# Attention: turned probabilities leave PSUM two chunks at a time, through two buffers of two banks in place of four of one

## What is computed

```
for blk in range(S // Q_BLOCK):                      # 16 blocks of 128 queries
    q0, q1 = blk * 128, blk * 128 + 128
    s = einsum("bhqd,bhkd->bhqk", q[:, :, q0:q1], k[:, :, :q1])
    s = s + cum[:, :, q0:q1, None] - cum[:, :, None, :q1]
    p = softmax(where(causal, s, -inf), axis=-1)
    outs.append(einsum("bhqk,bhkd->bhqd", p, v[:, :, :q1]))
```

## Time and profile before

| | |
|---|---|
| Median of three runs | 2558.09 us |
| Profiled execution, its own time | 2556.05 us |
| Its span, first to last instruction | 2553.9 us |
| Instructions | 37956 |
| TensorE matmul busy | 2409.2 us, 94% |
| TensorE weight load busy | 2081.5 us, 82% |
| DVE busy | 1352.8 us, 53% |
| ACT busy | 1150.0 us, 45% |
| POOL busy | 622.7 us, 24% |
| Mean granted TensorE clock | 0.974 |
| L828 on DVE, 640 instructions | 370.7 us busy |
| L773 on ACT, 640 instructions | 311.5 us busy |
| L692 on TensorE, 2176 instructions | 338.3 us busy |

### The profile page before, as it was taken

How to read it: one execution, slowest core, us unless ns; L and a number is a source line. 1 busy time by engine, 2 the same in 40 slices (tenths; PEclk the granted TensorE clock), 3 DMA queues, 4 the chain that set the end, 5 groups by cost and what they waited for, 6 DMA issues and landing times. The chain is left out here.

```text
span 2553.9 us, 37956 instructions
## 1 busy us (share of the span) xinstructions
PE 2409.2 (94%) x13921; PEld 2081.5 (82%) x13921; DVE 1352.8 (53%) x2844; ACT 1150.0 (45%) x2132; POOL 622.7 (24%) x739
## 2 busy tenths in 40 slices
PE   8999999999989999999999999699699999992997
PEld 7888889998868888888888888587488888872886
DVE  4232121211017888888888888453336656575443
ACT  2131111111117888888888888400035556565100
POOL 0010000000003554555545555244300000000254
PEclk9999999999998999999999999899899999996999
DMA  6434443332116455444554444455344444444653
GB/s 209 122 91 124 124 124 113 119 108 91 66 61 136 98 122 131 104 98 98 128 128 102 97 99 96 147 203 194 124 153 122 142 144 132 139 125 139 236 193 132
DMA packets 219999, 326.62 MB, mean 128 GB/s; under 512 B 17052, under 2 KB 144092, under 8 KB 213996
## 3 DMA queue, kind: packets, MB, share of 16 engines
q1 hardware_dynamic: 219304, 323.68, 44.3%
q0 software_dynamic: 512, 0.53, 0.1%
HBM read 197.79 MB, written 126.35 MB: 127 GB/s over the span
## 5 line engine op out<-in xcount | busy, mean ns | idle before, releaser
L828 DVE TENSOR_TENSOR at_pl<-at_tps,at_ph 128x512 fp32r<-128x512 f32 (+3 forms) x640 | 370.7, 604 | 30.1 <-ACT at_ph L773 30.1
L773 ACT ACTIVATE at_ph<-at_tps 128x512 fp32r<-128x512 f32 (+3 forms) x640 | 311.5, 527 | 114.5 <-PE at_tps L692 107.4
L323 ACT ACTIVATE pa_stg<-pa_ps 128x512 fp32r<-128x512 f32 (+1 forms) x128 | 76.5, 598 | 634.9 <-PE pa_ps L250 634.9
L692 PE MATMUL at_tps<-at_ident,at_probs 128*128 128x128 f32 x2176 | 338.3, 274 | 0.2 <-DVE at_pl L828 0.2
L710 PE MATMUL at_ops<-at_ph,at_val 128*128 128x256 f32 (+1 forms) x1152 | 325.5, 305 | 2.1 <-DVE at_pl L828 0.5
L763 ACT ACTIVATE at_probs<-at_probs,at_least 128x128 f32<-128x128 f32 (+15 forms) x256 | 307.2, 1200 | 9.1 <-DVE at_probs L819 9.0
L250 PE MATMUL pa_ps<-pa_xh,pa_wh 128*128 128x512 f32 x768 | 299.8, 390 | 3.8 <-DVE pa_wl L376 3.8
L250 PE MATMUL pa_ps<-pa_xh,pa_wl 128*128 128x512 f32 x768 | 298.9, 389 | 0.0
L250 PE MATMUL pa_ps<-pa_xl,pa_wh 128*128 128x512 f32 x768 | 298.8, 389 | 0.0
L710 PE MATMUL at_ops<-at_pl,at_val 128*128 128x256 f32 (+1 forms) x1152 | 295.0, 281 | 0.0
L677 PE MATMUL at_sps<-at_k,at_q 128*128 128x512 f32 (+3 forms) x640 | 272.9, 426 | 19.9 <-DMA at_k<-forget_sums 15.8
(11 more groups left out here) (172 smaller groups left out, 4645.4 us busy)
## 6 DMA issues: line engine op xcount, KB each, us to landing
at_q<-q_halves SPq DMA_DIRECT2D x45, 512.0 KB
at_k<-k_halves SPq DMA_DIRECT2D x45, 512.0 KB
q_halves<-pa_stg SPq DMA_DIRECT2D x32, 512.0 KB, 3.8
k_halves<-pa_stg SPq DMA_DIRECT2D x32, 512.0 KB, 3.7
v_halves<-pa_stg SPq DMA_DIRECT2D x32, 512.0 KB, 2.8
y_gated<-rep_work SPq DMA_DIRECT2D x32, 512.0 KB, 2.9
at_val<-v_halves SPq DMA_DIRECT2D x15, 1024.0 KB, 17.4
pa_wst<-in_attn_w_in SPq DMA_DIRECT2D x14, 1024.0 KB, 7.2
```

Of the source, the lines that this page charges most:

```text
L692: mm = nc.tensor.transpose(tps[c % TB][:, k, :], probs[s % ROWS][:, t0:t0 + P], ident[:, :])
L773: nc.scalar.activation(ph[g % 2][:, j * PB:j * PB + n, i % 2 * P:(i % 2 + 1) * P], tps[c % TB][:, 0:n, :], ACT.Copy).then_inc(high_out, 1)
L828: nc.vector.tensor_tensor(pl[g % 2][at], tps[c % TB][:, 0:n, :], raw(ph[g % 2][at]), ALU.subtract)\
```

## The change

A span is two chunks of a row, up to 1024 keys and eight tiles, and has one PSUM buffer of two banks; there are two such buffers in place of four of one bank. A row has one span (rows 0 to 7) or two (rows 8 to 15): 24 a head, 48 a pair. TensorE turns the tiles chunk by chunk in the same order as before, but it waits for the buffer once per span and counts `turned` up at the end of a span. `high` and `low` each handle a whole span in one instruction. DVE's order in a step changes: takes have the keys 0, 2, 4, 6 and lows 3, 7, so with four chunks it is take 0, take 1, low 0, take 2, take 3, low 1. The waits that counted chunks of `turned`, `high_out` and `low_out` count spans. The wait of the queue that loads a head is written in another way and has the same value.

```diff
+    n_spans = [(n + 1) // 2 for n in n_chunks]
+    first_span = [sum(n_spans[:s]) for s in range(STEPS)]
+    SPANS = sum(n_spans)
-    SB, TB = 2, 4
+    SB, TB = 2, 2
...
+    def span_tiles(s, j):
+        return min(2 * PB, s % QT + 1 - 2 * j * PB)
...
-        tps = [a.ps(f"tps{i}", [P, PB, P]) for i in range(TB)]
+        tps = [a.ps(f"tps{i}", [P, 2 * PB, P]) for i in range(TB)]
...
-                wait(sp, scored, chunks_before(it, QT * (hp + 1)) - CH if hp == 0 else it * CH)
+                wait(sp, scored, it * CH - CH // 2 if hp == 0 else it * CH)
...
-                c = first[s] + j
-                wait(pe, low_out, it * CH + c - TB + 1)
+                c = first_span[s] + j // 2
+                if j % 2 == 0:
+                    wait(pe, low_out, it * SPANS + c - TB + 1)
                 for k in range(width(s, j) // P):
                     t0 = (j * PB + k) * P
-                    mm = nc.tensor.transpose(tps[c % TB][:, k, :], probs[s % ROWS][:, t0:t0 + P], ident[:, :])
-                mm.then_inc(turned, 1)
+                    mm = nc.tensor.transpose(tps[c % TB][:, j % 2 * PB + k, :], probs[s % ROWS][:, t0:t0 + P], ident[:, :])
+                if j % 2 == 1 or j + 1 == n_chunks[s]:
+                    mm.then_inc(turned, 1)
...
-                    wait(pe, low_out, it * CH + first[2 * g + 1] + n_chunks[2 * g + 1])
+                    wait(pe, low_out, it * SPANS + first_span[2 * g + 1] + n_spans[2 * g + 1])
...
-                c, n = first[s] + j, width(s, j) // P
-                wait(act, turned, it * CH + c + 1)
-                nc.scalar.activation(ph[g % 2][:, j * PB:j * PB + n, i % 2 * P:(i % 2 + 1) * P],
+                c, n = first_span[s] + j, span_tiles(s, j)
+                wait(act, turned, it * SPANS + c + 1)
+                nc.scalar.activation(ph[g % 2][:, 2 * j * PB:2 * j * PB + n, i % 2 * P:(i % 2 + 1) * P],
                                      tps[c % TB][:, 0:n, :], ACT.Copy).then_inc(high_out, 1)
...
-                at(TURN_LAG, lambda t, n: [high(t, n, j) for j in range(n_chunks[n])])
+                at(TURN_LAG, lambda t, n: [high(t, n, j) for j in range(n_spans[n])])
...
-                    wait(dve, turned, chunks_before(it, s - ROWS + 1))
+                    wait(dve, turned, spans_before(it, s - ROWS + 1))
...
-                c, n = first[s] + j, width(s, j) // P
-                wait(dve, high_out, it * CH + c + 1)
-                at = (slice(None), slice(j * PB, j * PB + n), slice(i % 2 * P, (i % 2 + 1) * P))
+                c, n = first_span[s] + j, span_tiles(s, j)
+                wait(dve, high_out, it * SPANS + c + 1)
+                at = (slice(None), slice(2 * j * PB, 2 * j * PB + n), slice(i % 2 * P, (i % 2 + 1) * P))
...
-                turns = n_chunks[t_s] if turning else 0
-                for k, (second, j) in enumerate(alternate(scores_now, turns, 1)):
+                turns = n_spans[t_s] if turning else 0
+                order = sorted([(2 * j, False, j) for j in range(scores_now)]
+                               + [(4 * j + 3, True, j) for j in range(turns)])
+                for k, (_, second, j) in enumerate(order):
```

More of the change, by code:

```diff
@@ L481, in attend, with spans_before @@
     SKIP = 3
-    SB, TB = 2, 4
-    assert CH % SB == 0 and CH % TB == 0 and GROUPS % 4 == 0
-    def chunks_before(it, s):
-        return it * CH + first[s] if s >= 0 else it * CH - CH + first[s + STEPS]
+    SB, TB = 2, 2
+    assert CH % SB == 0 and SPANS % TB == 0 and GROUPS % 4 == 0
+    def spans_before(it, s):
+        return it * SPANS + first_span[s] if s >= 0 else it * SPANS - SPANS + first_span[s + STEPS]
+    def span_tiles(s, j):
+        return min(2 * PB, s % QT + 1 - 2 * j * PB)
     def width(s, j):
```

## The result

| | before | after |
|---|---|---|
| Median | 2558.18 us (4 runs) | 2611.24 us (4 runs) |
| Ratio | 1 | 1.0206, 95% interval 1.0188 to 1.0223 |
| Profiled execution, own time | 2556.05 us | 2607.12 us |
| Span | 2553.9 us | 2605.0 us |
| Attention, first to last matmul | 857.07 us | 908.67 us |

The change makes the kernel 53 us slower by the medians. Forecast were 2601 us, 43 us slower, in a range of 2578 to 2618. In the two traces attention grows by 51.6 us and the span by 51.1: the loss lies there and nowhere else.

What follows compares the result with a forecast made beforehand. TensorE, busy 94% of the span, was taken to bound the kernel. Terms a to h summed to +2.69 us a head, +43 us over 16 heads, giving 2601 us in a range of 2578 to 2618.

Steps and rivals of the forecast that it cites:

- Rival 1: Fewer instructions shorten the queue before takes, and TensorE's waits of 1.3 us a head go: at best 2537 us; 7%.
- rival 3: The wide instructions cost like two narrow ones: 2612 us, inside the range; 10% of the chance is there.
- Rival 2: Only the end of a head hurts (e to g): 2585 us; 12%.
- a: Step 12, first transposes: wait for the first wide low of step 11 to free the buffer, +0.5 us a head.
- b: Step 13, first score: waits for the third take of step 12, delayed behind a wide low, +0.36 us a head.
- c: Step 14, first score: waits likewise for the third take of the step before, +0.13 us a head.
- d: Step 16, third chunk's transposes: wait for the second low of step 15, +0.1 us a head.
- e: Step 17, first transposes: wait for step 16's first low, late through ACT's chain from step 15's exponential, +1.1 us a head.
- f: Step 18, first transposes: wait for the first low of step 17, +0.1 us a head.
- g: Step 19, weigh: waits for all of row 15, whose last wide high and low end later, +0.5 us a head.
- h: Step 8, third score: waits less for takes, -0.1 us a head.
- rival 4: TensorE's clock falls: steps 16 to 19 at half clock, up to 14 us a head, 2700 us and more; 3%.

Runs made afterwards that it cites:

- DVE's order alone: The kernel before, four one-bank buffers and narrow instructions, but with DVE's take and low order as in the change: 2573.36 us, ratio 1.0063.
- the layout: The kernel before with turned chunks in two buffers of two banks, high and low per chunk, each bank freed by its own low: 2564.17 us, ratio 1.0028.
- the release by span: The run with the layout, but TensorE waits for the lows of both chunks of a span before refilling the buffer: 2615.34 us, ratio 1.0225.

## Why the prediction was right, and by how much each step

The direction and the mechanism were right, and so were the places: but for 0.03 us in step 10 the waits came in the steps that the sum named. The total was 10 us short, 0.64 us a head.

**What bounds it.** That TensorE carries the stage and that its waits alone count held: DVE and ACT became less busy and the kernel slower. The relief, 0.07 us for each merged L, was 0.08: the take after a wide L at 1132.86 comes at 1134.00, 1.14 us later, against twice 0.61. It showed only in step 8, 0.06 for 0.1. Rival 1, which rested on relief, did not come.

The 0.125 us a pair that the prediction worked out from the Trainium skill's page "VectorE: DVE Perf Modes" (TRN2 errata) was not seen from start to start, where 0.08 is saved. By the same page an L of 1024 would take 1.19 us, an estimate; the trace has 1.222.

**The other rivals.** The measured 2611 is nearly the 2612 of rival 3, but not by its mechanism: wide instructions that cost like two would take 1.29 and 1.08 us, and they took 1.222 and 1.023. The time alone could not have told the two apart. Rival 2 had only the end of a head hurt; steps 11 to 14 hold 1.26 of the 3.33 us.

DVE in steps 11 and 12 of the changed kernel, to be read against the earlier trace rows:

```profile
1132.86 1.22 DVE L837 TENSOR_TENSOR at_pl<-at_tps,at_ph 128x1024 fp32r<-128x1024 f32 x1
1134.00 0.74 DVE L828 TENSOR_SCALAR_CACHE_REDUCE at_probs<-at_sps,at_least 128x512 f32<-128x512 f32 x1
...
1135.46 0.69 DVE L828 TENSOR_SCALAR_CACHE_REDUCE at_probs<-at_sps 128x512 f32<-128x512 f32 x1 [0.51 <-PE at_sps L685]
...
1136.96 1.22 DVE L837 TENSOR_TENSOR at_pl<-at_tps,at_ph 128x1024 fp32r<-128x1024 f32 x1
1138.09 0.74 DVE L828 TENSOR_SCALAR_CACHE_REDUCE at_probs<-at_sps,at_least 128x512 f32<-128x512 f32 x1
```

**a, step 12's t0:** 0.66 for 0.5. L ends at 1134.08 and the transposes start at 1134.23, 0.15 later where I had put 0.06: the first transposes of a step have two waits (see the last section). 0.06 more is s1 of step 11 waiting for T2 of step 10, which I had called just in time and priced at nothing.

**b and c, the takes behind a wide L:** 0.60 for 0.49 in steps 12 to 14. From s0 to s0, as the sum went, step 12 to 13 grew by 0.36 us for the 0.36 of b, and 13 to 14 by 0.23 for the 0.13 of c: c was the term that was short. T2 of step 12 ends at 1138.84 and s0 of step 13 starts at 1138.90, TensorE's weight load:

```profile
1138.29 0.42 PEld L700 LDWEIGHTS at_tps<-at_ident,at_probs 128*128 128x128 f32 x4 [0.18 <-issue]
1138.90 0.19 PEld L684 LDWEIGHTS at_sps<-at_k,at_q 128*128 128x128 f32 x1 [0.19 <-DVE at_probs L828]
```

There are two waits, 0.18 us ahead of t0, since L0 of step 12 ends at 1138.18, and 0.19 ahead of s0. The prediction named the second alone; its 0.36 us is right for both together, since it counts from s0 to s0. DVE's order alone shows the second by itself.

**d and e, step 16 and the transposes of step 17:** 1.28 for 1.2. The largest term was right; d was too small by 0.2 and e too large by 0.1, which partly cancel. t2 of step 16 waits 0.51 us for 0.21 before, so 0.3 more where I had 0.1: counted from the start of step 16, the take in front of this L starts 0.16 us later than before, and the L has 640 elements in place of 512 and takes 0.82 us for 0.69. t0 of step 17 waits 1.0 where I had 1.1.

```profile
1153.84 0.31 PEld L700 LDWEIGHTS at_tps<-at_ident,at_probs 128*128 128x128 f32 x3 [0.51 <-DVE at_pl L837]
...
1157.10 0.42 PEld L700 LDWEIGHTS at_tps<-at_ident,at_probs 128*128 128x128 f32 x4 [1.02 <-issue]
```

That the chain begins at the exponential of step 15 was shown by putting it earlier: 1.0 us of step 16 went.

**f, step 18's t0:** 0.30 for 0.1, with d the term most off. The sum had H of step 17 start when t1 is turned, 1.4 us after t0, and this is what happened; but it was 1.48 us (H at 1158.61, idle 0.21 us for TensorE, against t0 at 1157.13), and L0 ended 3.76 us after t0 where the sum has 3.66. The other half is the release: t0 of step 18 starts at 1161.04, 0.15 us after L0's end at 1160.89, where I had 0.06. The same 0.09 us are missing in a. ACT, DVE and the weight load at this place:

```profile
1158.61 1.03 ACT L782 ACTIVATE at_ph<-at_tps 128x1024 fp32r<-128x1024 f32 x1 [0.21 <-PE at_tps L700]
...
1159.67 2.41 DVE L837 TENSOR_TENSOR at_pl<-at_tps,at_ph 128x1024 fp32r<-128x1024 f32 x2 [0.95 <-ACT at_ph L782]
...
1161.01 0.42 PEld L700 LDWEIGHTS at_tps<-at_ident,at_probs 128*128 128x128 f32 x4 [0.27 <-issue]
```

The DVE row merges two L's; the first of them ends at 1160.89.

**g, weigh in step 19:** 0.50 for 0.5. **h:** right in sign.

**The clock** stayed at 1.00 in the head, so rival 4 did not come: the longest of the new waits was 1.1 us.

How soon a bank comes back decided: with narrow L the layout costs 7 us and the release by span 51 more. The Trainium skill's rule of rotating groups through PSUM banks (page "Perfetto Trace Analysis", Optimizing Tensor Performance, Matmuls) held in both kernels and could not tell them apart.

## What to carry to other kernels

When the engine that carries a stage is fed through a ring of buffers, merging two evacuations saves overlap on the evacuating engines and lengthens the way of each buffer. Before merging, read at each refill how long before it the freeing instruction ended; where that is less than the added time (here 0.5 us of L, 0.4 of H) the merge is paid by the engine that has no time. If the release must be coarse, do not let other work in between the reads that free a buffer (the wide L in its new order was worth 23 us here, nearly all of the shorter way due to the order by the times of single instructions). And an instruction that does not need the late half should not stand behind the one that does (6 us, in the kernel before).

## What had not been expected of the hardware

Where an instruction on TensorE has one wait, its weight load starts 0.05 to 0.06 us after the end it waited for (T2 ends 1138.84, load 1138.90; L ends at 1153.78, load 1153.84). The first transposes of a step wait for the exponential and for the buffer; the buffer's wait is an instruction of its own ahead of the load, and the load starts 0.11 to 0.12 us after L's end: 1138.18 to 1138.29, 1134.08 to 1134.20, 1156.98 to 1157.10. In the trace of the changed kernel the load starts 0.115 to 0.116 us after L's end at all 68 waits of this kind, and the loads that had a single wait for an L or a take start 0.052 to 0.054 us after its end. The trace of the kernel before has it too: L ends at 1137.65 and the load of step 18 starts at 1137.77, so the 0.06 us of the prediction could have been read better. This is also why the weight load's row there says "issue" or names ACT: the wait that took the time is not the load's own. That the extra instruction is the reason for the 0.06 us is argued from these places; no run took it away.
